# Two transformer blocks on one core: residual additions of seven rows on GpSimd, a leading weight chunk split in halves, and one copy moved to ScalarE

## The chip, the cores and the metric

The kernel runs on one core of a Trainium2 chip. The metric is the device time of one execution in microseconds (us). Before the change it is 1349.7 us, the median of three runs (1349.34 to 1349.88).

## What is computed

A residual stream x of 512 tokens by 1024 features goes through two blocks. Each block is a mixer and a feed-forward part, and both of them end and begin in the same way:

```python
x = x + gt_a * rms_norm(mix, g_mix_post)          # residual
h_ffn = modulate(rms_norm(x, g_ffn_pre), sh_f, sc_f)   # h * (1 + scale) + shift
ffn = conv_ffn(h_ffn, ...)
x = x + gt_f * rms_norm(ffn, g_ffn_post)
```

The first block mixes by retention and a Fourier transform, the second by a causal convolution and stick-breaking attention. All of it is fp32; the modulation vectors (shift, scale, gate) come from two matrix-vector products with 6144 columns each.

## The kernel before

Data is feature-major: a tile is 128 features by 512 tokens, and x (`xT`) is eight such tiles, k = 0 to 7. A matmul in fp32 precision is made of three rounded ones: each operand is split into a high part (`hH`, `WH`) and the rest (`hL`, `WL`). Weights come in a stream of chunks of 128 by 2048 into three slots. SP issues the load of a chunk when the matmuls of the chunk three places earlier are done. ScalarE makes `WH` (`split_hi`), VectorE makes `WL` (`split_lo`), and TensorE waits for `lo_done`. GpSimd issues the DMAs of the modulation weights (`ada_half`, two buffers, L335), which VectorE consumes in `ada_step`.

The change is about the three places, called boundaries here (m = 0, 1, 2), where one part's output y (eight tiles, written by TensorE into four banks in turn) is normed, added to x, and x is normed again as the input of the next part. The code takes the second norm's mean square from sums of y*y, (gain*y)^2 and gain*y*x, so that it needn't wait for the new x:

- In the last tiles of the output phase (`out_tile`) VectorE copies gain*y to `yT` (L1166), multiplies by x (L1169) and adds to three sums (L1174, L1178). For tile 7 it makes only gain*y*x (L1162) and then `yT` (L1163), behind ScalarE's square of the bank (L606). Between tiles 6 and 7 both engines split the second chunk of the next phase (`split_hi`, `split_lo` of c0+5 or c0+13), 2048 columns at once.
- TensorE's `late_stats` sums over features (L1521), spreads the first root to all partitions (L1528, bank 4), later the second root (L1528, bank 5), and between them runs matmuls whose result nobody reads (`keep_running`, L1782, bank 7). It first waits for `mod_read`.
- ScalarE makes the first root from bank 4 (`y_root`, L382 and L383) and, once VectorE has made `sxx` (L1195 to L1200), the second.
- VectorE's `boundary` then scales y by the first root, reading bank 4 (`scale_y`, L1185), and adds it to x (`add_x`, L1189). The loop over k runs: L1212 (x times gain times second root, reading bank 5, to `tmp1`), `scale_y(k + 2)`, `add_x(k + 1)`, then, after ScalarE has made `hH` of tile k (L647), L1218 for `hL`. At its end the third chunk is split in four parts (L837).
- TensorE's `lead` multiplies two chunks at once, tile by tile as `hH` and `hL` come: per k eight matmuls with `hH` (L1814, L1815) and four with `hL` (L1820). It first waits for both chunks (`have(c + 1)`).

Each engine runs its instructions in program order; the order above is written out by hand, with semaphores between engines.

Of the kernel before, what the change touches and what calls it, by code (L numbers as in the profile page):

```python
# [21 lines left out]
KT = D // P  # L22
# [12 lines left out]
CH = 2048  # L35
# [56 lines left out]
def build(nc, weights, ada, ada_later, x_t, ctx_t, vecs, rope, band, pos, csd, masks, sel, x_rows, gain_row, out):  # L92
# [4 lines left out]
    with stack:  # L97
# [221 lines left out]
        @block.gpsimd  # L319
        def _(pool):  # L320
            pool.dma_start(selT[:, :], sel).then_inc(s.sel_in, 16)
            nc.gpsimd.memset(csil_pair[:, :, :], 0.0).then_inc(s.const_set, 1)
            nc.gpsimd.memset(eps[:, :], EPS).then_inc(s.const_set, 1)
            nc.gpsimd.memset(ones[:, :], 1.0).then_inc(s.const_set, 1)
            nc.gpsimd.memset(lift[:, :], 0.0).then_inc(s.const_set, 1)
            nc.gpsimd.memset(gp3[:, :], 0.0).then_inc(s.const_set, 1)
            pool.wait_ge(s.const_set, 5)
            for q in range(4):
                nc.gpsimd.memset(lift[32 * q:32 * q + 1, q:q + 1], 1.0).then_inc(s.const_set, 1)

            pool.wait_ge(s.mod0_sum, ADA_FIRST)
            for a in range(STEPS):
                if a >= 2:
                    pool.wait_ge(s.ada_read, a - 1)
                pool.dma_start(ada_half[:, a % 2, :], ada_later[a]).then_inc(ada_in[a % 2], 16)  # L335

            for p in range(PAIRS):
                if p % 4 in (1, 2):
                    w = P * (p % 4 + 1)
                    for e in range(2):  # L340
                        pool.wait_ge(s.sp_lo, 2 * p + e + 1)
                        if p % 4 == 2:
                            pool.wait_ge(s.cum_sum, passed(p - 1) - 1 + e)
                        nc.gpsimd.tensor_tensor(spF[p % 2][:, e, P:w], spF[p % 2][:, e, P:w],
                                                spF[(p - 1) % 2][:, e, 0:w - P], add).then_inc(s.cum_sum, 1)

            pool.wait_ge(s.turned, 1)
            for q in range(4):
                pool.dma_start(gain_row.rearrange("(k q j) -> q k j", q=4, j=32)[q], gpT[32 * q:32 * q + KT, :])\
                    .then_inc(s.rows_out, 16)  # L350
            pool.wait_ge(s.rows_out, 64)
            pool.dma_start(gpB[:, :], gain_row.partition_broadcast(P)).then_inc(s.rows_in, 16)
            for k in range(KT):
                pool.wait_ge(s.turned, k + 2)
                blocks = xB[:, k % 4, :].rearrange("p (b j) -> p b j", j=32)
                for q in range(4):
                    at = slice(P * k + 32 * q, P * k + 32 * q + 32)
                    pool.dma_start(x_rows[:, at].rearrange("(b i) j -> i b j", i=32), blocks[32 * q:32 * q + 32, :, :])\
                        .then_inc(s.rows_out, 16)
                pool.wait_ge(s.rows_out, 64 * (k + 2))  # L360
            pool.wait_ge(s.mm_done, 16 * C_DOWN2)
            pool.dma_start(x_tok[:, :, :], x_rows.rearrange("(t p) c -> p t c", p=P)).then_inc(s.rows_in, 16)

        @block.scalar
        def _(act):
# [3 lines left out]
            def split_hi(c, width=CH):  # L369
                slot = c % SLOTS  # L370
                act.wait_ge(raw_in[slot], 16 * (c // SLOTS) + 16)
                A(WH[:, slot, 0:width], raw[:, slot, 0:width], ACT.Copy).then_inc(s.hi_done, 1)  # L372
# [224 lines left out]
            def out_squares(m, n, done_at):  # L597
# [9 lines left out]
                if n < KT - 1:  # L607
                    A(to[:, 1, :], b[:, :], ACT.Square, scale=gp[:, n:n + 1]).then_inc(s.zz_ready, 1)

            def out_phase(m, c0):  # L610

                pin_ln_exp()
                split_hi(c0 + 1)
                for p in range(4):
                    if p < 3:
                        split_hi(c0 + p + 2)
                    out_squares(m, 2 * p, done(c0 + p, 0, 2))
                    if p == 3:
                        split_hi(c0 + 5)
                    out_squares(m, 2 * p + 1, done(c0 + p, 1, 2))  # L620

            def down_phase(m, c0):
                pin_ln_exp()
                for p in range(4):
                    for j in range(3):
                        q = 3 * p + j
                        if q < 11:
                            split_hi(c0 + q + 2)
                    out_squares(m, 2 * p, done(c0 + 3 * p + 2, 0, 2))
                    if p == 3:  # L630
                        split_hi(c0 + 13)
                    out_squares(m, 2 * p + 1, done(c0 + 3 * p + 2, 1, 2))

            def y_root(m):
# [3 lines left out]
            def next_norm(m, c0):  # L638

                y_root(m - 1)  # L640
                act.wait_ge(s.sxx_ready, m + 1)
                inverse_root(xroot, sxx[:, :], 1.0 / D, s.xroot_ready)
                for k in range(KT):
                    if k == 4:
                        split_hi(c0 + 2)
                    act.wait_ge(s.norm_mul, m * KT + k + 1)
                    A(hH[:, k, :], tmp1[:, k % 4, :], ACT.Identity, bias=mod[:, SHIFT_AT[m] + k:SHIFT_AT[m] + k + 1])\  # L647
                        .then_inc(s.h_hi, 1)
# [173 lines left out]
        def _(dve):  # L822
# [333 lines left out]
            def out_tile(m, n, free0):  # L1156

                if n == KT - 1:
                    b = bank[Y_BANKS[m][n % 4]]
                    dve.wait_ge(s.yy_ready, m * KT + n + 1)  # L1160
                    dve.wait_ge(s.xy_added, 6 * m + 6)
                    STT(last_xy[m][:, :], b[:, :], gp[:, n:n + 1], xT[:, n, :], mult, mult).then_inc(s.xy_ready, 1)  # L1162
                    TS(yT[:, n, :], b[:, :], gp[:, n:n + 1], None, mult).then_inc(s.bank_free, 1)  # L1163
                    return
                dve.wait_ge(s.zz_ready, m * (KT - 1) + n + 1)
                TS(yT[:, n, :], bank[Y_BANKS[m][n % 4]][:, :], gp[:, n:n + 1], None, mult).then_inc(s.bank_free, 1)  # L1166
# [10 lines left out]
                        dve.wait_ge(s.xy_added, 6 * m + n - 1)  # L1177
                    TT_(sums[m][:, 2, :], sums[m][:, 2, :], xy, add).then_inc(s.xy_added, 1)  # L1178

            def boundary(m, c0):  # L1180

                r, r2, t = bank[4][:, :], bank[5][:, :], xsum

# [4 lines left out]
                    dve.wait_ge(s.y_scaled, KT * m + k + 1)  # L1188
                    TT_(xT[:, k, :], xT[:, k, :], yT[:, k, :], add).then_inc(s.x_new, 1)  # L1189

                at = SCALE_AT[m + 1]
                STT(gm[:, 0, :], mod[:, at:at + KT], 1.0, v(f"g{m + 1}", 0, KT), add, mult).then_inc(s.gm_ready, 1)
                dve.wait_ge(s.root_ready, m + 1)
                dve.wait_ge(s.zstat_done, m + 1)
                own.link(TT_(t, bank[5][:, 0:P], yroot, mult))  # L1195
# [4 lines left out]
                TS(sxx[:, :], sxx[:, :], 0.0, None, ALU.max).then_inc(s.sxx_ready, 1)  # L1200
                dve.wait_ge(s.y_spread, m + 1)
                scale_y(0)
                scale_y(1)
                add_x(0)
                dve.wait_ge(s.gm_ready, m + 1)
                dve.wait_ge(s.x_spread, m + 2)
                at = SHIFT_AT[m + 1]
                for k in range(KT):
                    dve.wait_ge(s.x_new, KT * m + k + 1)
                    if k >= 4:  # L1210
                        dve.wait_ge(s.h_lo, KT * (m + 1) + k - 3)
                    STT(tmp1[:, k % 4, :], xT[:, k, :], gm[:, 0, k:k + 1], r2, mult, mult).then_inc(s.norm_mul, 1)  # L1212
                    if k < KT - 2:
                        scale_y(k + 2)
                    if k < KT - 1:
                        add_x(k + 1)
                    dve.wait_ge(s.h_hi, KT * (m + 1) + k + 1)
                    STT(hL[:, k, :], tmp1[:, k % 4, :], mod[:, at + k:at + k + 1], hH[:, k, :], add, sub)\  # L1218
                        .then_inc(s.h_lo, 1)
                split_lo_parts(c0 + 2, m)  # L1220

            def out_phase(m, c0, free0, after, steps=(0, 0, 0, 0)):
                post_gain(m)
                split_lo(c0 + 1)
                for p in range(4):
                    if p < 3:
                        split_lo(c0 + p + 2)
                        ada_steps(steps[p])
                    out_tile(m, 2 * p, free0)
                    if p == 3:  # L1230
                        split_lo(c0 + 5)
                        if m == 0:
                            modulation(2, 8, 24)
                    out_tile(m, 2 * p + 1, free0)
                boundary(m, after)

            def down_phase(m, c0, free0, after):
                post_gain(m)
                for p in range(4):
# [6 lines left out]
                                modulation(4, 40, 48)  # L1246
                    out_tile(m, 2 * p, free0)
                    if p == 3:
                        split_lo(c0 + 13)
                    out_tile(m, 2 * p + 1, free0)  # L1250
                boundary(m, after)

            out_phase(0, C_OUT, B_OUT, C_UP, (1, 1, 0, 0))
            assert ada_next[0] == STEPS_UP, ada_next
# [215 lines left out]
        def _(pe):  # L1470
# [313 lines left out]
            def late_stats(m):  # L1784

                have((C_UP, C_U, C_UP2)[m])
                pe.wait_ge(s.mod_read, (2, 5, 6)[m])
                early_stats(m)
                pe.wait_ge(s.yy_ready, (m + 1) * KT)
                token_sums(4, odd_sq[m][:, 0, :], False, True).then_inc(s.ystat_done, 1)  # L1790
                pe.wait_ge(s.gp_squared, m + 1)
                token_sums(5, odd_sq[m][:, 0, :], False, True, gp_last[:, 0:1].to_broadcast([P, 32]))\
                    .then_inc(s.zstat_done, 1)
                keep_running(m, 2)
                pe.wait_ge(s.xy_ready, (m + 1) * KT)
                token_sums(6, last_xy[m][:, :], False, True).then_inc(s.xystat_done, 1)
                pe.wait_ge(s.const_set, 9)
                pe.wait_ge(s.root_ready, m + 1)
                spread(4, yroot).then_inc(s.y_spread, 1)
                keep_running(m, 4)  # L1800
                pe.wait_ge(s.xroot_ready, m + 2)
                spread(5, xroot).then_inc(s.x_spread, 1)
                keep_running(m, 5)

            def lead(c, banks, at):

                have(c + 1)
                for k in range(KT):
                    pe.wait_ge(s.h_hi, at + k + 1)
                    for j in range(2):  # L1810
                        for x in range(2):
# [378 lines left out]
```

## Time and profile before

| | |
|---|---|
| median of three runs | 1349.7 us |
| profiled execution, its own time | 1348.56 us |
| its span in the trace | 1346.8 us |
| PE busy | 1327.9 us, 99% |
| VectorE busy | 901.4 us, 67% |
| ScalarE busy | 526.4 us, 39% |
| GpSimd busy | 83.8 us, 6% |
| granted TensorE clock | 9 tenths or more of full speed in all 40 slices |

Engines are named PE (TensorE matmul), PEld (its weight load), DVE (VectorE), ACT (ScalarE), POOL (GpSimd) and SP. Matmul ends are modelled, so a busy PE is not PE at its peak. The three boundaries lie at about 264 to 295 us, 633 to 662 us and 974 to 1005 us of the span. What matters there is which engine is waited for last, and that is read from the timeline.

### The profile page before, as it was taken

To read this page: it belongs to the slowest core of one execution; us is meant where nothing else is said; L and a number is where in the kernel's file an instruction comes from. 1 tells how busy PE (TensorE), PEld (TensorE's weight loads), DVE (VectorE), ACT (ScalarE), POOL (GpSimd) and SP (SyncE) were. 2 spreads that over 40 slices of the span, in tenths; PEclk is the share of its full clock that TensorE was granted. 3 is DMA by queue.
4 is the path that set the end of the run, shared out by engine and by line. 5 is a ranking of instruction groups with operands and counts; after the bars stand their busy time and mean duration, and the time that the engine had idled before them with its cause. 6 is when DMAs were issued, how large, how long until landed. Compare 5 with 4: busy or idle time off the path is not lost.

```text
span 1346.8 us, 15738 instructions
## 1 busy us (share of the span) xinstructions
PE 1327.9 (99%) x6461; PEld 1077.6 (80%) x6461; DVE 901.4 (67%) x1126; ACT 526.4 (39%) x747; POOL 83.8 (6%) x148
## 2 busy tenths in 40 slices
PE   7999999999999999999999999999999999999998
PEld 4799688778888888887888777778878888888886
DVE  4787878988777777678758899766875433332224
ACT  4552444344334443222422666774333222222112
POOL 0000001000000001010000100000002220000000
PEclk9999999999999999999999999999999999999999
DMA  9543046324445555654123211112224332224331
GB/s 390 191 141 126 17 155 220 125 78 175 163 162 196 171 183 186 217 202 173 71 94 98 90 64 63 63 63 96 98 86 131 116 115 94 94 98 161 107 104 63
DMA packets 32887, 176.47 MB, mean 131 GB/s; under 512 B 4128, under 2 KB 4400, under 8 KB 17840
## 3 DMA queue, kind: packets, MB, share of 16 engines
q1 hardware_dynamic: 19440, 128.78, 26.7%
q0 software_dynamic: 13376, 46.69, 10.8%
q8 instruction: 51, 0.84, 0.3%
q14 instruction: 20, 0.16, 0.0%
HBM read 171.26 MB, written 4.20 MB: 130 GB/s over the span
## 4 chain that ended last, share of the span: by engine, by line
PE 90%; DVE 5%; issue 2%; ACT 2%; DMA 2%; SPq 0%; DVEq 0%; ACTq 0%
PE bank L1475 27%; PE bank L1477 26%; PE bank L1476 26%; PE bank L1814 2%; PE bank L1815 2%; PE bank L1820 2%; PE bank L1680 1%; DMA adaf<-ada 1%; PE bank L2010 1%; PE bank L1980 1%; DVE WL L830 1%; DVE sums L1174 1%; PE bank L1998 1%; PE bank L1997 1%; DMA raw<-weights 1%
## 5 line engine op out<-in xcount | busy, mean ns | idle before, releaser
L1475 PE MATMUL bank<-hH,WH 128*128 128x512 f32 x992 | 390.1, 393 | 0.9 <-DVE WL L830 0.6
L830 DVE TENSOR_TENSOR WL<-raw,WH 128x2048 fp32r<-128x2048 f32 x103 | 234.5, 2278 | 230.2 <-ACT WH L372 230.2
L1477 PE MATMUL bank<-hH,WL 128*128 128x512 f32 x992 | 386.4, 390 | 0.0
L1476 PE MATMUL bank<-hL,WH 128*128 128x512 f32 x992 | 386.2, 389 | 0.0
L372 ACT ACTIVATE WH<-raw 128x2048 fp32r<-128x2048 f32 x106 | 201.5, 1904 | 237.3 <-DMA raw<-weights 237.3
L1475 PEld LDWEIGHTS bank<-hH,WH 128*128 128x128 f32 x992 | 186.3, 188 | 42.6 <-issue 3.3
L1477 PEld LDWEIGHTS bank<-hH,WL 128*128 128x128 f32 x992 | 186.2, 188 | 39.6
L1476 PEld LDWEIGHTS bank<-hL,WH 128*128 128x128 f32 x992 | 186.3, 188 | 37.6 <-issue 0.2
L859 DVE SCALAR_TENSOR_TENSOR ada_acc<-ada_half,csil,ada_acc 128x1024 f32<-128x1024 f32 x70 | 89.7, 1281 | 6.4 <-DMA ada_half<-ada_later 3.8
L1307 DVE SCALAR_TENSOR_TENSOR cacc<-uT,vec,cacc 128x511 f32<-128x511 f32 (+29 forms) x120 | 83.3, 755 | 0.0
L335 POOL DMA_DIRECT2D ada_half<-ada_later x80 | 42.4, 530 | 571.8 <-DVE ada_acc L859 333.4
L1475 PE MATMUL bank<-GH,WH 128*128 128x512 f32 x176 | 68.7, 390 | 0.0
L1477 PE MATMUL bank<-GH,WL 128*128 128x512 f32 x176 | 68.5, 389 | 0.0
L1476 PE MATMUL bank<-GL,WH 128*128 128x512 f32 x176 | 68.5, 389 | 0.0
L1475 PE MATMUL bank<-WH,GH 128*128 128x512 f32 x176 | 68.5, 389 | 0.0
L1476 PE MATMUL bank<-WL,GH 128*128 128x512 f32 x176 | 68.5, 389 | 0.0
L1477 PE MATMUL bank<-WH,GL 128*128 128x512 f32 x176 | 68.5, 389 | 0.0
L806 ACT ACTIVATE GH<-tB 128x512 fp32r<-128x512 f32 x22 | 13.9, 632 | 88.5 <-DVE tB L1446 88.5
L1265 DVE SCALAR_TENSOR_TENSOR tB<-bank,vec,tB 128x504 f32<-128x504 f32 x22 | 16.4, 743 | 40.8 <-ACT tB L660 40.7
L660 ACT ACTIVATE tB<-bank,vec 128x512 f32<-128x512 f32 x22 | 17.2, 780 | 67.0 <-PE bank L1477 67.0
L1814 PE MATMUL bank<-hH,WH 128*128 128x512 f32 x96 | 37.6, 392 | 1.8 <-ACT hH L647 1.8
L1475 PEld LDWEIGHTS bank<-WH,GH 128*128 128x128 f32 x176 | 33.0, 188 | 6.9
(333 smaller groups left out, 2075.1 us busy)
## 6 DMA issues: line engine op xcount, KB each, us to landing
raw<-weights SPq DMA_DIRECT2D x108, 1024.0 KB, 4.9
ada_half<-ada_later POOLq DMA_DIRECT2D x80, 512.0 KB, 4.4
adaf<-ada SPq DMA_DIRECT2D x8, 1024.0 KB, 19.8
xT<-x_t SPq DMA_DIRECT2D x4, 512.0 KB, 5.7
x_rows<-xB POOLq DMA_DIRECT2D x32, 64.0 KB, 2.2
x_tok<-x_rows POOLq DMA_DIRECT2D x1, 2048.0 KB, 10.9
out_t<-x_tok SPq DMA_DIRECT2D x8, 256.0 KB, 2.0
ctxT<-ctx_t SPq DMA_DIRECT2D x1, 1024.0 KB, 28.6
```

The costliest lines, as they stand in the source:

```text
L335: pool.dma_start(ada_half[:, a % 2, :], ada_later[a]).then_inc(ada_in[a % 2], 16)
L372: A(WH[:, slot, 0:width], raw[:, slot, 0:width], ACT.Copy).then_inc(s.hi_done, 1)
L660: A(tmp[:, j, :], bank[2 * (t % 3) + x][:, :], ACT.Identity, bias=v("cb", x * FT + t), scale=v("cw", 2 * FT + x * FT + t)).then_inc(s.conv ...
L830: TT_(WL[:, slot, 0:width], raw[:, slot, 0:width], WH[:, slot, 0:width], sub).then_inc(s.lo_done, 1)
L859: ins = STT(ada_acc[:, :], w, c_col, ada_acc[:, :], mult, add)
L1307: STT(cacc[:, k, shift:L], uT[:, k, 0:L - shift], w, cacc[:, k, shift:L], mult, add)\
L1475: mm(o, lh, rh, start=start, stop=False, skip_group_check=skip)
L1476: mm(o, lh, rl, start=False, stop=False, skip_group_check=skip)
L1477: return mm(o, ll, rh, start=False, stop=stop, skip_group_check=skip)
L1814: mm(o, wh, hH[:, k, :], start=(k == 0), stop=False)
L1815: mm(o, wl, hH[:, k, :], start=False, stop=False)
L1820: ins = mm(bank[banks[j] + x][:, :], wh, hL[:, k, :], start=False, stop=(k == KT - 1))
```

## The change

It has four parts.

1. `add_x(k)` for k = 1 to 7 leaves VectorE and is issued by GpSimd (`residual(m)`), each behind `y_scaled` of its tile. `residual(0)` stands in GpSimd's queue behind the issue of the modulation DMA 25, `residual(1)` behind the last of them, `residual(2)` ahead of the DMAs of the gain row. VectorE keeps `add_x(0)`, now ahead of `scale_y(1)`.
2. The second leading chunk is split in halves: ScalarE makes both halves where it made the whole; VectorE makes half 0 between tiles 6 and 7 and half 1 in the loop at k = 2, ahead of `hL` of that tile. `lead` waits for half 0 at its start, for the whole at k = 4.
3. The copy `yT` of tile 7 goes to ScalarE, behind its first root, and VectorE waits for it at k = 5.
4. `gm` is made before tile 7; TensorE's wait for `mod_read` comes after the sums, and two of its filler matmuls are gone.

```diff
+            def residual(m):
+                for k in range(1, KT):
+                    pool.wait_ge(s.y_scaled, KT * m + k + 1)
+                    nc.gpsimd.tensor_tensor(xT[:, k, :], xT[:, k, :], yT[:, k, :], add).then_inc(s.x_new, 1)
...
                 pool.dma_start(ada_half[:, a % 2, :], ada_later[a]).then_inc(ada_in[a % 2], 16)
+                if a == STEPS_UP + 1:
+                    residual(0)
+            residual(1)
...
+            residual(2)
             pool.wait_ge(s.turned, 1)
...
+            def lead_hi(c):
+                slot = c % SLOTS
+                act.wait_ge(raw_in[slot], 16 * (c // SLOTS) + 16)
+                for half, ready in enumerate((s.hi_half, s.hi_done)):
+                    at = slice(CH // 2 * half, CH // 2 * half + CH // 2)
+                    A(WH[:, slot, at], raw[:, slot, at], ACT.Copy).then_inc(ready, 1)
...
                 y_root(m - 1)
+                n = KT - 1
+                act.wait_ge(s.xy_ready, m * KT)
+                A(yT[:, n, :], bank[Y_BANKS[m - 1][n % 4]][:, :], ACT.Identity, scale=gp[:, n:n + 1])\
+                    .then_inc(s.bank_free, 1)
                 act.wait_ge(s.sxx_ready, m + 1)
...
                     STT(last_xy[m][:, :], b[:, :], gp[:, n:n + 1], xT[:, n, :], mult, mult).then_inc(s.xy_ready, 1)
-                    TS(yT[:, n, :], b[:, :], gp[:, n:n + 1], None, mult).then_inc(s.bank_free, 1)
...
+            def lead_lo(m, c, half):
+                slot = c % SLOTS
+                at = slice(CH // 2 * half, CH // 2 * half + CH // 2)
+                if half:
+                    dve.wait_ge(s.hi_done, c + 1)
+                else:
+                    dve.wait_ge(s.hi_half, 2 + m + 1)
+                TT_(WL[:, slot, at], raw[:, slot, at], WH[:, slot, at], sub).then_inc(s.lo_done if half else s.lo_half, 1)
...
                 scale_y(0)
+                add_x(0)
                 scale_y(1)
-                add_x(0)
...
+                    if k == KT - 3:
+                        dve.wait_ge(s.bank_free, free0 + KT)
                     if k < KT - 2:
                         scale_y(k + 2)
-                    if k < KT - 1:
-                        add_x(k + 1)
+                    if k == 2:
+                        lead_lo(m, c0 + 1, 1)
                     dve.wait_ge(s.h_hi, KT * (m + 1) + k + 1)
...
                     if p == 3:
-                        split_lo(c0 + 5)
                         if m == 0:
                             modulation(2, 8, 24)
+                        next_gain(m)
+                        lead_lo(m, after + 1, 0)
...
-                pe.wait_ge(s.mod_read, (2, 5, 6)[m])
                 early_stats(m)
...
-                keep_running(m, 2)
+                pe.wait_ge(s.mod_read, (2, 5, 6)[m])
+                keep_running(m, 1)
...
-                keep_running(m, 4)
+                keep_running(m, 3)
...
-                have(c + 1)
+                have(c)
+                pe.wait_ge(s.lo_half, 2 + at // KT)
                 for k in range(KT):
+                    if k == 4:
+                        have(c + 1)
                     pe.wait_ge(s.h_hi, at + k + 1)
```

## Rows read from the trace of the kernel before

**Rows 1.** Timeline, boundary 1: start us, us, engine line op, operands, [idle before <-releaser].
```profile
632.12 2.29 DVE L830 TENSOR_TENSOR WL<-raw,WH 128x2048 fp32r<-128x2048 f32 x1
...
633.22 0.60 ACT L606 ACTIVATE odd_sq<-bank 128x512 f32<-128x512 f32 x1 [2.45 <-PE bank L1477]
...
634.32 0.74 DVE L1162 SCALAR_TENSOR_TENSOR last_xy<-bank,gp,xT 128x512 f32<-128x512 f32 x1
...
634.76 0.31 ACT L383 ACTIVATE rstd<-rstd 128x128 f32<-128x128 f32 x1
...
635.71 0.28 DVE L1195 TENSOR_TENSOR rstd<-bank,rstd 128x128 f32<-128x128 f32 x1
...
637.01 0.23 DVE L1200 TENSOR_SCALAR sxx<-sxx 128x128 f32<-128x128 f32 x1
...
638.07 1.16 PE L1528 MATMUL bank<-rstd,lift 128*128 128x128 f32 x8 [0.50 <-ACT rstd L383]
...
640.98 0.47 PE L1814 MATMUL bank<-hH,WH 128*128 128x512 f32 x1 [0.59 <-ACT hH L647]
```

**Rows 2.** Timeline, boundary 0, where the wait for the modulation lies.
```profile
264.05 0.60 ACT L606 ACTIVATE odd_sq<-bank 128x512 f32<-128x512 f32 x1 [2.88 <-PE bank L1477]
...
265.33 0.17 DVE L880 TENSOR_TENSOR mod<-bank,vec 128x16 f32<-128x16 f32 x1
...
269.04 0.23 DVE L1200 TENSOR_SCALAR sxx<-sxx 128x128 f32<-128x128 f32 x1
```

**Rows 3.** Timeline, boundary 2, the same line as in rows 1.
```profile
978.20 0.23 DVE L1200 TENSOR_SCALAR sxx<-sxx 128x128 f32<-128x128 f32 x1
```

**Rows 4.** Timeline, boundary 0, VectorE's loop over k.
```profile
276.41 0.74 DVE L1212 SCALAR_TENSOR_TENSOR tmp<-xT,gm,bank 128x512 f32<-128x512 f32 x1
...
277.07 0.68 DVE L1185 TENSOR_TENSOR yT<-yT,bank 128x512 f32<-128x512 f32 x1
...
278.27 0.74 DVE L1218 SCALAR_TENSOR_TENSOR hL<-tmp,mod,hH 128x512 fp32r<-128x512 f32 x1
...
286.50 0.74 DVE L1212 SCALAR_TENSOR_TENSOR tmp<-xT,gm,bank 128x512 f32<-128x512 f32 x1
...
288.03 0.75 DVE L1218 SCALAR_TENSOR_TENSOR hL<-tmp,mod,hH 128x512 fp32r<-128x512 f32 x1 [0.19 <-ACT hH L647]
```

**Rows 5.** Chain that ended last, boundary 0: start us, us, what.
```profile
273.01 0.47 PE bank L1814
...
275.10 0.92 PE bank L1820 x4
...
277.83 0.91 PE bank L1820 x4
```

**Rows 6.** Timeline, attention stage: GpSimd's additions of 256 columns beside VectorE.
```profile
769.63 3.19 POOL L344 TENSOR_TENSOR spF<-spF,spF 128x256 f32<-128x256 f32 x1 [5.66 <-DVE spL L1349]
769.95 2.28 DVE L830 TENSOR_TENSOR WL<-raw,WH 128x2048 fp32r<-128x2048 f32 x1
...
858.00 0.69 DVE L1409 TENSOR_TENSOR cacc<-cacc,rstd 128x512 f32<-128x512 f32 x1
...
865.28 0.56 DVE L1349 TENSOR_TENSOR spL<-spF,spH 128x384 fp32r<-128x384 f32 x1
...
865.76 0.55 DVE L1349 TENSOR_TENSOR spL<-spF,spH 128x384 fp32r<-128x384 f32 x1
865.92 0.99 POOL L344 TENSOR_TENSOR spF<-spF,spF 128x256 f32<-128x256 f32 x1 [9.14 <-DVE spL L1349]
866.23 1.23 DVE L1374 TENSOR_TENSOR lnsq<-lnsq 128x512 f32<-128x512 f32 x1
```

**Rows 7.** Timeline, attention stage: additions of 128 columns beside a cast from PSUM.
```profile
792.80 0.42 DVE L1349 TENSOR_TENSOR spL<-spF,spH 128x256 fp32r<-128x256 f32 x1
...
792.97 0.58 POOL L344 TENSOR_TENSOR spF<-spF,spF 128x128 f32<-128x128 f32 x1 [19.01 <-DVE spL L1349]
...
793.50 0.46 POOL L344 TENSOR_TENSOR spF<-spF,spF 128x128 f32<-128x128 f32 x1
```

More of the change, by code:

```diff
@@ L618, in out_phase @@
                     if p == 3:
-                        split_hi(c0 + 5)
+                        lead_hi(c0 + 5)
                     out_squares(m, 2 * p + 1, done(c0 + p, 1, 2))
@@ L630, in down_phase @@
                     if p == 3:
-                        split_hi(c0 + 13)
+                        lead_hi(c0 + 13)
                     out_squares(m, 2 * p + 1, done(c0 + 3 * p + 2, 1, 2))
@@ L1178, in out_tile, with next_gain, boundary @@
                     TT_(sums[m][:, 2, :], sums[m][:, 2, :], xy, add).then_inc(s.xy_added, 1)
-            def boundary(m, c0):
+            def lead_lo(m, c, half):
[6 more added lines that the diff above has]
+                TT_(WL[:, slot, at], raw[:, slot, at], WH[:, slot, at], sub).then_inc(s.lo_done if half else s.lo_half, 1)
+            def next_gain(m):
+                at = SCALE_AT[m + 1]
+                STT(gm[:, 0, :], mod[:, at:at + KT], 1.0, v(f"g{m + 1}", 0, KT), add, mult).then_inc(s.gm_ready, 1)
+            def boundary(m, c0, free0):
                 r, r2, t = bank[4][:, :], bank[5][:, :], xsum
@@ L1189, in add_x @@
                     TT_(xT[:, k, :], xT[:, k, :], yT[:, k, :], add).then_inc(s.x_new, 1)
-                at = SCALE_AT[m + 1]
-                STT(gm[:, 0, :], mod[:, at:at + KT], 1.0, v(f"g{m + 1}", 0, KT), add, mult).then_inc(s.gm_ready, 1)
                 dve.wait_ge(s.root_ready, m + 1)
@@ L1230, in out_phase @@
                     if p == 3:
-                        split_lo(c0 + 5)
                         if m == 0:
                             modulation(2, 8, 24)
+                        next_gain(m)
+                        lead_lo(m, after + 1, 0)
                     out_tile(m, 2 * p + 1, free0)
-                boundary(m, after)
+                boundary(m, after, free0)
             def down_phase(m, c0, free0, after):
@@ L1248, in down_phase @@
                     if p == 3:
-                        split_lo(c0 + 13)
+                        next_gain(m)
+                        lead_lo(m, after + 1, 0)
                     out_tile(m, 2 * p + 1, free0)
-                boundary(m, after)
+                boundary(m, after, free0)
             out_phase(0, C_OUT, B_OUT, C_UP, (1, 1, 0, 0))
```

## Prediction

> **What bounds the kernel now.** I read the page first: PE is busy 99% of the span, so only a place where PE waits can give time. The chain of waits shows three alike, the boundaries; the timeline around each is what counts. At boundary 1 [rows 1] the reader is to follow one chain: the square of tile 7 (starts 633.22, lasts 0.60), the last product L1162 (634.32), L1195 to L1200 on VectorE (635.71 to 637.01 plus 0.23), the second root on ScalarE, its spread on PE (638.07, 1.16), L1212, `hH`, and the first matmul of `lead` at 640.98. Behind that PE goes without a stop: one k of `lead` takes 277.83 - 275.10 = 2.73 us [rows 5]. VectorE's loop is just inside that: L1212, `scale_y` 0.66 later, an addition of about 0.60, `hL` 1.86 after L1212, and 0.66 more for `hL`, 2.52 us a k [rows 4].
>
> **Part 1: the chain ahead of `lead`.** Half of the 2.29 us split goes from ahead of tile 7. At boundary 1 VectorE is then free at 632.12 + 1.15 + 0.10 for `gm` = 633.4, and L1162 waits for the square: 633.82 + 0.06 = 633.88 in place of 634.32, done 634.62. L1195 no longer stands behind the copy of tile 7 but behind the first root: 634.76 + 0.31 + 0.03 = 635.10 in place of 635.71 [rows 1]. That is 0.61 us, and it carries to L1200, the second root and the spread. Boundary 2 has the same pattern (L1200 at 978.20) [rows 3]: 0.62 us. At boundary 0 the modulation's read L880 stood behind the split, at 265.33, and PE's sums and the first root behind it. With the wait moved, the square (264.05 + 0.60) is followed by the sums as in boundary 1: L1200 starts 637.01 - 635.71 = 1.30 after L1195, L1195 starts 635.10 - 633.22 = 1.88 after the square starts, so 264.05 + 1.88 + 1.30 = 267.23 against 269.04, a gain of 1.8 us [rows 1, 2]. The three sum to 3.0 us.
>
> What could take the place: ScalarE's copy of tile 7 costs some 0.70 us (my estimate, its square takes 0.60) from 635.10, and the second root is wanted at 637.27 - 0.61 = 636.66; so 0.86 us of cover is left, and the copy costs nothing. PE's first spread begins with the first root, 635.14, ends by 636.3, and VectorE wants it at 636.54; three fillers fit ahead of 637.46. VectorE's `scale_y(0)`, `add_x(0)`, `scale_y(1)`, now in series, end about 2.0 us later, 638.54, ahead of L1212 (638.72). Without these covers each would cost its own length. ScalarE's split in two instructions costs 0.2 us inside 2.45 or 2.88 us of idle time [rows 1, 2]: nothing. GpSimd's queue: DMA 26 waits for the tile loop behind boundary 0, the last modulation DMAs are issued before boundary 1, and the gain row comes from VectorE after boundary 2; nothing waits behind `residual`.
>
> **Part 2: the loop.** VectorE loses seven additions, and without other effects one k takes 1.53 us from L1212 to `hL` (288.03 - 286.50) and 0.66 for `hL`, 2.19 us [rows 4]. PE's 2.73 would still be the bound, and `hL`'s half split (1.15 us at k = 2) would fit.
>
> But the additions are not gone. The trace shows what a GpSimd addition does to a VectorE instruction with both inputs in SBUF: the 512-column addition L1374 lasts 1.23 us in place of the 0.69 of L1409, ending 0.55 after GpSimd's ends (866.91 to 867.46), and GpSimd's own began only when the L1349 ahead of it ended (866.31) [rows 6]. One stands still while the other runs. `hL` (from `tmp1` and `hH`) is such an instruction, and so are both split halves; L1212 and `scale_y` read one SBUF tensor and a bank. How long GpSimd holds: 0.60 us for 256 columns (866.31 to 866.91), 0.33 for 128 (793.22 to 793.55), so 512 columns give an estimate of 0.60 + 2 x 0.27 = 1.14 us [rows 6, 7]. No row shows 512 columns; the bounds are 0.69 (VectorE's speed) and 4 x 0.46 = 1.84.
>
> Who comes first decides. Count from the start of L1212(k). `scale_y(k + 2)` starts at 0.66 and ends at 1.34 [rows 4]; GpSimd follows the end of a VectorE instruction by 0.08 (865.84 to 865.92) [rows 6], so its addition is issued at 1.42. `hL(k)` is issued at 1.53. GpSimd leads by 0.11 us in every k from 0 to 5. It needs about 0.13 us before it begins (793.96 - 0.33 - 793.50) [rows 7], and VectorE needs part of 0.15, the excess of 0.69 over 512 columns, so this is close. I take GpSimd as first: it is issued first, and in rows 6 it goes ahead of L1374, issued 0.31 after it. The same rows hold the contrary case: at 769.63 GpSimd was issued 0.32 ahead of L830, yet lasted 3.19, behind all of L830's 2.28.
>
> If GpSimd is first, it ends at 1.55 + 1.14 = 2.69, `hL` at 3.24, and the next L1212 starts at 3.17: VectorE is the bound, 0.44 us a k above PE's 2.73. At k = 2 the half split holds till 2.48, GpSimd runs to 3.63, `hL` ends at 4.18, and the k takes 4.09: 1.36 above. First k: PE's own is some 0.2 longer (275.10 + 0.92 - 273.01 = 3.01 by the chain, 2.84 by the timeline), so only 0.25 is lost. A boundary loses 0.25 + 0.44 + 1.36 + 3 x 0.44 = 3.4 us, three 10.2, and with the 3.0 gained the change costs **7.2 us**.
>
> The Trainium skill, SBUF — State Buffer, section Who interferes with whom, says that a VectorE instruction with two SBUF inputs and a GpSimd one that reads SBUF exclude each other, and that whichever is issued first has the ports for its whole length. By that rule GpSimd is first and the time is the forecast below; by the row at 769.63 it may lose, and the time would be the first rival's.
>
> **How the numbers follow.** The profiled execution took 1348.56 us, 1.8 more than its span; 7.2 more is 1355.8. The median is 1.1 above the profiled one, so **1356.9 us**, slower by 0.5%. With the hold between 0.69 and 1.84 us a k changes by -0.45 to +0.70: the forecast's own range is 1348 to 1370, and 1354 to 1359 where the estimate holds within 0.15 us. Chance 0.58.
>
> **Rival A, VectorE first.** `hL` takes the ports from 1.53, GpSimd waits some 0.7 us and runs beside the next L1212 and `scale_y`, whose banks it doesn't touch; its sum is due a whole k later. A k takes 2.19, PE's 2.73 bounds, even with the split half and ScalarE's split at k = 4 (each delays VectorE by under 1.2 us, against 0.5 us of lead won in every k). The 3.0 us stay: 1346.7. For it: the row at 769.63 and the close race. Against it: 0.11 us of lead. Chance 0.27. It is the case on the other side, and decides where GpSimd begins over 0.11 us later than I read.
>
> **Rival B, mixed.** GpSimd is first in some k only, or only at k = 2 is VectorE's `hL` the first behind the half split. The latter takes 1.1 us from each boundary: 1353.6. If GpSimd wins no more than every second k, the lead VectorE gains in the others (0.54 each) covers most of the loss: 1348 to 1351. Together 0.15.
>
> **Rival C, the change doesn't shorten the chain**, since the spread or the copy is later than I read. It lowers the gain of 3.0 by under 1 us and is held in the ranges of the others.
>
> **Chances.** A measurement of this kernel can tell about 0.2%, 2.7 us, from no change. Rival A, 3.0 us faster, lies barely beyond: 0.22 of it faster, 0.05 the same. B gives 0.10 the same, 0.02 faster and 0.03 slower, the forecast 0.58 slower. So faster 0.24, same 0.15, slower 0.61. The range 1346.3 to 1359 takes in all three cases and leaves out a longer hold of GpSimd.
>
> **What would show it.** In the changed kernel, L1200's place should start 1.8, 0.6 and 0.6 us sooner after the last matmul of the phase. GpSimd's additions should show 1.3 us or more, `hL` of k = 0 to 5 about 1.7 us in place of 0.74, the first L1814 of k = 1 to 6 idle ahead of it 0.3 to 1.4 us, and a `lead` of about 25 us for 21.9. If `hL` shows 0.74 and GpSimd's additions about 2 us, rival A holds. The forecast is wrong too if a VectorE instruction that reads a bank and one SBUF tensor is held up: then every k costs more.

## The result, and the profile after

The changed kernel takes 1357.12 us (median of five runs, 1355.98 to 1357.71). Against runs of the kernel before on the same chip the ratio is 1.0058, with a 95% interval of 1.0044 to 1.0072: slower by 0.6%, about 7.8 us. The profiled execution has a span of 1354.6 us for 1346.8.

Two lines of the page of the changed kernel show where to look, and so do PE's waits in the lead (us in total, times, longest), first of the changed kernel, then of the kernel before:

```profile
PE 1333.4 (98%) x6455; PEld 1075.4 (79%) x6455; DVE 906.6 (67%) x1105; ACT 528.6 (39%) x753; POOL 113.9 (8%) x169
...
L335 POOL TENSOR_TENSOR xT<-xT,yT 128x512 f32<-128x512 f32 x21 | 29.8, 1420 | 185.3 <-DVE yT L1222 185.3
```

```profile
PE bank L1856 <- ACT hH L670: 3.1, 9, 0.6
PE bank L1862 <- DVE hL L1255: 1.7, 3, 0.6
```

```profile
PE bank L1814 <- ACT hH L647: 1.8, 3, 0.6
```

VectorE has 21 instructions less and GpSimd 21 more, and yet VectorE is busy 5 us longer. In the leads PE waits for `hH` in nine places where it waited in three, and three times for `hL`, for which it didn't wait there before.

The timeline of the changed kernel at boundary 0 answers rows 1, 2 and 4. The chain ahead of `lead`, from the square of tile 7:

```profile
262.99 1.22 DVE L1210 TENSOR_TENSOR WL<-raw,WH 128x1024 fp32r<-128x1024 f32 x1
264.22 0.60 ACT L617 ACTIVATE odd_sq<-bank 128x512 f32<-128x512 f32 x1 [2.78 <-PE bank L1516]
...
265.98 0.67 ACT L662 ACTIVATE yT<-bank,gp 128x512 f32<-128x512 f32 x1
266.10 0.29 DVE L1230 TENSOR_TENSOR rstd<-bank,rstd 128x128 f32<-128x128 f32 x1 [0.50 <-ACT rstd L394]
...
267.42 0.23 DVE L1235 TENSOR_SCALAR sxx<-sxx 128x128 f32<-128x128 f32 x1
```

L1235 (L1200 before) starts 3.20 us after the square where it started 269.04 - 264.05 = 4.99 after it [rows 2]: 1.8 us won. Then the loop over k, first k = 1, then k = 2 with the half split L1210, then the start of k = 3:

```profile
272.90 0.74 DVE L1247 SCALAR_TENSOR_TENSOR tmp<-xT,gm,bank 128x512 f32<-128x512 f32 x1
273.56 0.68 DVE L1222 TENSOR_TENSOR yT<-yT,bank 128x512 f32<-128x512 f32 x1
...
274.32 1.28 POOL L335 TENSOR_TENSOR xT<-xT,yT 128x512 f32<-128x512 f32 x1 [1.88 <-DVE yT L1222]
274.43 1.72 DVE L1255 SCALAR_TENSOR_TENSOR hL<-tmp,mod,hH 128x512 fp32r<-128x512 f32 x1 [0.20 <-ACT hH L670]
...
276.07 0.73 DVE L1247 SCALAR_TENSOR_TENSOR tmp<-xT,gm,bank 128x512 f32<-128x512 f32 x1
...
277.33 1.21 DVE L1210 TENSOR_TENSOR WL<-raw,WH 128x1024 fp32r<-128x1024 f32 x1
277.48 2.21 POOL L335 TENSOR_TENSOR xT<-xT,yT 128x512 f32<-128x512 f32 x1 [1.88 <-DVE yT L1222]
...
278.46 1.78 DVE L1255 SCALAR_TENSOR_TENSOR hL<-tmp,mod,hH 128x512 fp32r<-128x512 f32 x1
280.17 0.73 DVE L1247 SCALAR_TENSOR_TENSOR tmp<-xT,gm,bank 128x512 f32<-128x512 f32 x1
```

GpSimd's addition is issued 0.11 us ahead of `hL` (274.32, 274.43) and ends at 275.60; `hL` takes 1.72 us for 0.74 and ends at 276.15. One k takes 276.07 - 272.90 = 3.17 us, the k with the half split 280.17 - 276.07 = 4.10. L1247 and L1222, which read one SBUF tensor and a bank, are not held. At k = 0 an addition runs beside both, and all three take their usual time:

```profile
269.65 1.29 POOL L335 TENSOR_TENSOR xT<-xT,yT 128x512 f32<-128x512 f32 x1 [23.80 <-DVE yT L1222]
269.73 0.75 DVE L1247 SCALAR_TENSOR_TENSOR tmp<-xT,gm,bank 128x512 f32<-128x512 f32 x1 [0.17 <-PE bank L1567]
270.39 0.68 DVE L1222 TENSOR_TENSOR yT<-yT,bank 128x512 f32<-128x512 f32 x1
```

All runs can be laid out by three landmarks in each boundary: the square of tile 7, the first matmul of `lead`, and the end of its last group of four. "Gap" is from the first to the second, "lead" from the second to the third, in us of the profiled execution:

| kernel | gap 0, 1, 2 | lead 0, 1, 2 | span |
|---|---|---|---|
| before | 8.96, 7.76, 7.76 | 22.05, 22.05, 22.01 | 1346.8 |
| changed | 7.16, 7.16, 7.16 | 25.59, 25.60, 25.61 | 1354.6 |
| e1_adds_on_dve | 7.16, 7.16, 7.17 | 22.53, 22.51, 22.53 | 1345.8 |
| e2_after_hl | 7.16, 7.17, 7.16 | 22.06, 22.04, 22.03 | 1344.9 |
| e3_half_add | 7.16, 7.16, 7.16 | 22.65, 22.62, 22.60 | 1345.3 |
| e4_only_adds | 8.37, 7.76, 7.76 | 24.67, 24.66, 24.65 | 1354.0 |
| e5_delays | 7.16, 7.16, 7.16 | 25.63, 25.83, 25.98 | 1355.3 |
| e6_copy | 7.17, 7.16, 7.17 | 22.17, 22.22, 22.18 | 1345.8 |
| e7_write_only | 7.17, 7.16, 7.17 | 22.04, 22.01, 22.01 | 1344.8 |
| e8_copy_back | 7.21, 7.20, 7.22 | 22.01, 22.05, 22.01 | 1343.3 |
| e9_tie | 7.16, 7.17, 7.16 | 22.33, 22.30, 22.30 | 1345.5 |
| e10_only_adds_after_hl | 8.36, 7.76, 7.76 | 22.04, 22.01, 22.03 | 1346.2 |

For the changed kernel the gaps give back 1.80 + 0.60 + 0.60 = 3.0 us and the leads take 3.54 + 3.55 + 3.60 = 10.7; together 7.7 of the span's 7.8. What lies between the boundaries takes the same in both to 0.1 us; the stretch ahead of the first is 0.2 us longer. Each row of the table is one execution, and the gap of boundary 0 in the kernel before depends on the execution, as is shown further down.

### The profile page after: what moved, and what is told of

The parts are those of the page before. It is cut to its first block, busy times and chain, and to the rows that moved or that the text cites. A ratio compares the mean times of both kernels' runs of the same rounds, so it can differ in the third digit from the quotient of the medians.

```text
span 1354.6 us, 15738 instructions
## 1 busy us (share of the span) xinstructions
PE 1333.4 (98%) x6455; PEld 1075.4 (79%) x6455; DVE 906.6 (67%) x1105; ACT 528.6 (39%) x753; POOL 113.9 (8%) x169
## 4 chain that ended last, share of the span: by engine, by line
PE 84%; DVE 8%; ACT 4%; issue 2%; DMA 1%; SPq 0%; DVEq 0%; ACTq 0%
PE bank L1514 26%; PE bank L1515 26%; PE bank L1516 26%; DVE hL L1255 1%; DVE tmp L1247 1%; DMA adaf<-ada 1%; PE bank L1719 1%; ACT hH L670 1%; DVE ada_acc L882 1%; DVE WL L853 1%; PE bank L2052 1%; PE bank L2022 1%; ACT WH L383 1%; PE bank L2040 1%; PE bank L2039 1%
## 5 line engine op out<-in xcount | busy, mean ns | idle before, releaser
L853 DVE TENSOR_TENSOR WL<-raw,WH 128x2048 fp32r<-128x2048 f32 x100 | 227.6, 2278 | 230.6 <-ACT WH L383 230.5
L383 ACT ACTIVATE WH<-raw 128x2048 fp32r<-128x2048 f32 x103 | 195.7, 1903 | 235.9 <-DMA raw<-weights 235.8
L335 POOL TENSOR_TENSOR xT<-xT,yT 128x512 f32<-128x512 f32 x21 | 29.8, 1420 | 185.3 <-DVE yT L1222 185.3
```

Source lines behind the costliest of these rows:

```text
L335: nc.gpsimd.tensor_tensor(xT[:, k, :], xT[:, k, :], yT[:, k, :], add).then_inc(s.x_new, 1)
L853: TT_(WL[:, slot, 0:width], raw[:, slot, 0:width], WH[:, slot, 0:width], sub).then_inc(s.lo_done, 1)
```

## The experiments

**e1_adds_on_dve: the other three parts alone.**

```diff
-                if a == STEPS_UP + 1:
-                    residual(0)
-            residual(1)
-            residual(2)
...
                         scale_y(k + 2)
+                    if k < KT - 1:
+                        add_x(k + 1)
                     if k == 2:
```

> All parts of the change but the first: add_x(1) to add_x(7) are back on VectorE, in their old place behind scale_y(k + 2); GpSimd adds nothing. Theory (the loss is hL held up by GpSimd's additions): the chain ahead of lead keeps its 3.0 us; a k of VectorE's loop takes 2.52 us again, plus 1.15 us for the half split at k = 2, which the 0.2 us a k won on PE by then doesn't cover: about 0.3 us lost in each boundary. 1347.7 us, ratio to before 0.9985; hL shows 0.74 us everywhere. Rival (the halves, the copy on ScalarE or the moved waits are what costs): 1354 us or more.

Measured: 1347.64 us against 1348.45 for the kernel before, ratio 0.9995 (0.9987 to 1.0004). The gaps keep their 7.16 us, and the leads lose 0.5 us each, for the 0.3 expected. The rival is out by far: without GpSimd's additions none of the 7.8 us is left. The ratio was expected lower by 0.001; that is looked at below.

**e2_after_hl: GpSimd always second.**

```diff
                     pool.wait_ge(s.y_scaled, KT * m + k + 1)
+                    if k >= 2:
+                        pool.wait_ge(s.h_lo, KT * (m + 1) + k - 1)
                     nc.gpsimd.tensor_tensor(xT[:, k, :], xT[:, k, :], yT[:, k, :], add)...
```

> The changed kernel, but GpSimd's addition k waits, from k = 2 on, until hL(k - 2) is done; so GpSimd always comes second. Theory: each hL takes 0.74 us, a k of VectorE's loop 2.2 us, lead is bound by PE at 2.73 us a k and lasts 22.0 us for 25.6, and the 3.0 us of the chain remain: 1346.7 us, ratio 0.9978. Rival (GpSimd's additions are simply too slow, and L1247 waits for them): GpSimd starts even later here, so lead stays at 25 us or more and the time at 1357 us or above.

Measured: 1347.04 us, ratio to before 0.9989 (0.9980 to 0.9998): 1.5 us faster, and the 0.9978 expected lies just outside the interval. The timeline of this kernel, boundary 0, k = 1:

```profile
272.27 0.74 DVE L1249 SCALAR_TENSOR_TENSOR tmp<-xT,gm,bank 128x512 f32<-128x512 f32 x1
272.50 1.29 POOL L337 TENSOR_TENSOR xT<-xT,yT 128x512 f32<-128x512 f32 x1 [1.23 <-DVE hL L1257]
...
273.81 0.75 DVE L1257 SCALAR_TENSOR_TENSOR hL<-tmp,mod,hH 128x512 fp32r<-128x512 f32 x1 [0.19 <-ACT hH L672]
...
274.48 0.74 DVE L1249 SCALAR_TENSOR_TENSOR tmp<-xT,gm,bank 128x512 f32<-128x512 f32 x1
```

The same additions, just as long, now begin beside L1249 and end (273.79) when the next `hL` is issued. Only the half split at k = 2 still meets the end of one: it takes 1.35 us for 1.22. A k takes 2.21 us and lead 22.05. In the profile, one added wait on the helping engine takes all of the 10.7 us of the leads away; between the two ratios, 1.0058 and 0.9989, lie 9.3 us. The additions' own slowness cost nothing.

**e3_half_add: half the length of the hold.**

```diff
-   nc.gpsimd.tensor_tensor(xT[:, k, :], xT[:, k, :], yT[:, k, :], add)
+   nc.gpsimd.tensor_tensor(xT[:, k, 0:256], xT[:, k, 0:256], yT[:, k, 0:256], add)
```

> The changed kernel with GpSimd adding columns 0 to 255 of the seven tiles only; the residual is left out for the other 256 tokens in tiles 1 to 7. Theory (the loss is the length of the hold): the hold falls from 1.14 to 0.60 us, hL takes about 1.2 us, a k 2.6 us, inside PE's 2.73; only k = 2 with the half split still costs some 0.4 us a boundary: 1347.9 us, ratio 0.9987. Rival (a fixed cost of each GpSimd instruction or semaphore delays hL): the loss hardly falls, 1355 us or more.

Measured: 1348.03 us, ratio 0.9999 (0.9989 to 1.0008). Its timeline:

```profile
273.35 0.73 POOL L335 TENSOR_TENSOR xT<-xT,yT 128x256 f32<-128x256 f32 x1 [1.88 <-DVE yT L1222]
273.47 1.17 DVE L1255 SCALAR_TENSOR_TENSOR hL<-tmp,mod,hH 128x512 fp32r<-128x512 f32 x1 [0.20 <-ACT hH L670]
```

`hL` falls from 1.72 to 1.17 us with an addition that is 0.55 shorter: the loss is the length of the hold, not a fixed cost. A k takes 2.61 us (274.55 - 271.94), inside PE's 2.73. With the half split at k = 2 a lead is 22.6, a loss of 0.6 us for the 0.4 expected. The ratio was expected at 0.9987, a little below the interval.

**e4_only_adds: the first part alone.** The kernel before, with `residual(m)` on GpSimd and `add_x(1)` to `add_x(7)` gone from VectorE. One more line changes place: `add_x(0)` stands ahead of `scale_y(1)`, as in the changed kernel. It lies under cover: the gaps of boundaries 1 and 2 stay at 7.76 us.

```diff
+            residual(0) / residual(1) / residual(2)   # at the same places in GpSimd's queue
...
                 scale_y(0)
+                add_x(0)
                 scale_y(1)
-                add_x(0)
...
-                    if k < KT - 1:
-                        add_x(k + 1)
```

> The kernel before with only the seven additions moved to GpSimd: the split of the second chunk whole, the copy on VectorE, TensorE's waits and fillers as before. Theory: no gain in the chain, and in lead 0.25 us at k = 1 and 0.44 at k = 2 to 6, 2.45 us a boundary: 7.4 us slower, 1357.1 us, ratio 1.0055, lead 24.5 us in each boundary. Rival (the loss needs the half split inside the loop): about 1350 us, ratio 1.000.

Measured: 1356.57 us, ratio 1.0061 (1.0049 to 1.0074). Leads of 24.66 us, 2.6 more than before, 7.9 in sum. So the two ways in which the loss grows are apart now: 2.6 us a boundary from `hL` alone, 0.9 more from the half split that queues in the same loop (25.6 in the changed kernel).

**e5_delays: small memsets ahead of GpSimd's addition.**

```diff
+                    for e in range(m if k >= 2 else 0):
+                        at = 8 + 6 * (m - 1 + e) + k - 2
+                        nc.gpsimd.memset(gp3[:, at:at + 1], 0.0)
```

> The changed kernel with small GpSimd memsets of one column ahead of each addition from k = 2 on: none in boundary 0, one in boundary 1, two in boundary 2. A memset of that size takes about 0.1 us, so the addition is issued 1.42, 1.53 and 1.63 us after L1247, and hL at 1.53. Theory (who comes first decides, and GpSimd leads by 0.11 us): boundary 0 as in the changed kernel, hL 1.72 us and lead 25.6 us; boundary 2 tips over to VectorE, hL 0.74 us and lead about 22.1 us; boundary 1 lies on the edge. Rival (GpSimd wins whenever both are near, or wins over an instruction already running): all three leads stay at 25.6 us or grow with the memsets.

Measured: leads of 25.63, 25.83 and 25.98 us, 1357.06 us in one run. That boundary 2 would tip over was wrong, and the timeline says why: the memsets overlap, and two of them put the addition off by only 0.09 us (issued 986.57, from 986.48).

```profile
986.48 0.13 POOL L337 MEMSET gp<- 128x1 f32 x2 [0.21 <-DVE yT L1225]
986.57 1.29 POOL L338 TENSOR_TENSOR xT<-xT,yT 128x512 f32<-128x512 f32 x1
986.61 1.79 DVE L1258 SCALAR_TENSOR_TENSOR hL<-tmp,mod,hH 128x512 fp32r<-128x512 f32 x1 [0.19 <-ACT hH L673]
```

A lead of 0.04 us is still enough for GpSimd, and `hL` is held as long as GpSimd ends later. This run alone leaves open whether issue order decides or GpSimd wins every close race.

**e9_tie: the same event releases both.** It takes up that question. The edit is the wait below, with the memsets of e5 behind it.

```diff
+                    if k >= 2:
+                        pool.wait_ge(s.h_hi, KT * (m + 1) + k - 1)
```

> The changed kernel with GpSimd's addition k waiting, from k = 2 on, for ScalarE's hH(k - 2) as well, the same event that releases hL(k - 2); behind that wait stand no, one and two one-column memsets in boundaries 0, 1 and 2, each some 0.05 us by the last look. So GpSimd is issued at about the same time as hL, 0.05 and 0.1 us after it. Theory (the one that is issued first takes the reads): the lead turns from 25.6 us to about 22.1 us between one boundary and the next, where GpSimd's issue falls behind VectorE's; hL is 1.7 us or 0.75 us, nothing between. Rival (GpSimd wins every close race, VectorE's claim coming late in its instruction): all three boundaries stay at 25.6 us or more.

Measured: leads of 22.33, 22.30 and 22.30 us, 1347.29 us in one run. Neither side of the expectation holds as written: all three boundaries turned, since GpSimd answers ScalarE's event 0.12 us later than VectorE does, without any memset. What theory and rival disagree on is settled all the same:

```profile
271.55 0.75 DVE L1260 SCALAR_TENSOR_TENSOR hL<-tmp,mod,hH 128x512 fp32r<-128x512 f32 x1 [0.19 <-ACT hH L675]
...
271.67 1.79 POOL L340 TENSOR_TENSOR xT<-xT,yT 128x512 f32<-128x512 f32 x1 [0.44 <-ACT hH L675]
```

Issued 0.12 us behind `hL`, GpSimd is the one that stands still: 1.79 us for 1.29, while `hL` takes its 0.75. Between 0.04 us ahead (e5) and 0.12 us behind the order turns; where in between was not tried.

One k in each boundary did not turn, k = 2. There VectorE is still at its half split when ScalarE's event comes, so GpSimd's addition is issued ahead of `hL` again, and `hL` is held as in the changed kernel:

```profile
276.07 1.98 POOL L340 TENSOR_TENSOR xT<-xT,yT 128x512 f32<-128x512 f32 x1 [0.40 <-ACT hH L675]
...
276.82 1.78 DVE L1260 SCALAR_TENSOR_TENSOR hL<-tmp,mod,hH 128x512 fp32r<-128x512 f32 x1
```

That is where the leads lose the 0.26 to 0.27 us by which they are above e2's: PE's k = 2 and k = 3 take up to 2.88 us for 2.72, all others what they take in e2.

**e6_copy and e7_write_only: what is held.** GpSimd's addition gives way to a copy (one tensor read) and to a memset (none read).

```diff
-   nc.gpsimd.tensor_tensor(xT[:, k, :], xT[:, k, :], yT[:, k, :], add)
+   nc.gpsimd.tensor_copy(xT[:, k, :], yT[:, k, :])     # e6
+   nc.gpsimd.memset(xT[:, k, :], 1.0)                  # e7
```

> The changed kernel with GpSimd copying yT to xT in place of adding (the sum with the old x is left out for tiles 1 to 7): one tensor read in place of two. Theory (any GpSimd instruction that reads SBUF holds hL for its length): hL of k = 0 to 5 is still held, for as long as the copy lasts; if a copy takes half of the addition's 1.29 us, hL takes about 1.2 us and lead 22.6 us. Rival (only the second tensor read is in VectorE's way): hL 0.74 us, lead 22.1 us.

> The changed kernel with GpSimd filling tiles 1 to 7 of xT with ones by memset in place of adding (the residual and the old x are left out there): it reads nothing and writes 512 columns. Theory (what is shared is the way in which a second SBUF tensor is read): hL takes 0.74 us everywhere, the half split 1.22 us, lead 22.1 us. Rival (any GpSimd instruction on SBUF holds VectorE): hL is held by the memset's length, some 0.4 us.

Measured: 1347.86 us with the copy and 1346.76 with the memset, one run each. First the copy, then the memset, each at boundary 0:

```profile
272.19 0.61 POOL L335 COPY xT<-yT 128x512 f32<-128x512 f32 x1 [0.89 <-DVE yT L1222]
272.31 1.03 DVE L1255 SCALAR_TENSOR_TENSOR hL<-tmp,mod,hH 128x512 fp32r<-128x512 f32 x1 [0.19 <-ACT hH L670]
```

```profile
271.59 0.53 POOL L335 MEMSET xT<- 128x512 f32 x1 [0.98 <-DVE yT L1222]
271.73 0.75 DVE L1255 SCALAR_TENSOR_TENSOR hL<-tmp,mod,hH 128x512 fp32r<-128x512 f32 x1 [0.19 <-ACT hH L670]
```

The copy ends at 272.80 and `hL` 0.54 us later, at 273.34, as behind an addition; the memset, which runs beside `hL` for 0.39 us, leaves it at 0.75. Nor does VectorE hold the memset: beside the half split (275.85, 1.22 us) one issued at 275.99 takes 0.53 us as ever. So one read tensor is enough to hold VectorE, and a write is not. This is what the page SBUF — State Buffer of the Trainium skill says under Who interferes with whom, of both. Leads are 22.2 and 22.0 us; the copy was a little shorter than half the addition (0.61), so its 1.03 and 22.2 lie under the 1.2 and 22.6 expected.

**e8_copy_back: what of the other parts gave the chain's gain.** The kernel of e2, with two parts undone:

```diff
     STT(last_xy[m][:, :], b[:, :], gp[:, n:n + 1], xT[:, n, :], mult, mult).then_inc(s.xy_ready, 1)
+    TS(yT[:, n, :], b[:, :], gp[:, n:n + 1], None, mult).then_inc(s.bank_free, 1)
...
+                pe.wait_ge(s.mod_read, (2, 5, 6)[m])
                 early_stats(m)
```

> The kernel in which GpSimd's additions wait for hL(k - 2), with two more parts undone: the copy of tile 7 is on VectorE again, behind its last product, and TensorE again waits for mod_read ahead of its sums. Theory: the copy on VectorE ends 0.1 us after the first root, so the time from the last square to lead grows from 7.16 to 7.26 us in each boundary and no more; the wait for mod_read costs nothing, since the modulation's read now stands ahead of the half split, and boundary 0 shows the same 7.26. Rival (the copy's move is what the chain's gain comes from): 7.7 us. Rival (the wait is): 8 us or more in boundary 0 alone.

Measured: gaps of 7.21, 7.20 and 7.22 us, 1345.11 us in one run. The copy's move to ScalarE is worth 0.05 us a boundary, the moved wait nothing. What is left of the gain has not been taken apart by a run of its own, but VectorE's rows of boundary 1 show where it lies: the square, the last product and L1195's place start at 630.85, 631.48 and 632.80, in the kernel before at 633.22, 634.32 and 635.71. The product comes 0.47 us sooner behind the square (the half split) and L1195 0.07 us sooner behind the product (`gm` no longer stands between them). At boundary 0 the modulation's read, now ahead of the split, adds to it. The two fillers that are gone were not what was waited for in boundary 1: in the kernel before PE stood idle behind them for 0.50 us, waiting for the second root [rows 1].

**e10_only_adds_after_hl: the offload without the collision.** The kernel of e4, with e2's wait.

> The kernel before with only the seven additions moved to GpSimd, each from k = 2 on waiting for hL(k - 2). Theory: hL is no longer held, a k of VectorE's loop takes 2.2 us in place of 2.52, but PE's 2.73 was the bound already, so the move gives nothing: gaps of 7.76 us in boundaries 1 and 2, leads of 22.05 us, the time of the kernel before, ratio 1.000 within 0.001. Rival (taking work off VectorE is worth something by itself): leads below 22 us and a ratio of 0.998 or less.

Measured: 1348.55 us against 1348.16, ratio 1.0003 (0.9994 to 1.0013), leads of 22.04, 22.01 and 22.03. Taking seven additions off VectorE is worth nothing here, since PE's 2.73 us a k was the bound. The gap of boundary 0 is 8.36 us, as in e4 (8.37), for the 8.96 of the kernel before, though nothing ahead of the boundary is changed in either.

## Why the prediction was right, point by point

- **The chain ahead of lead, 3.0 us.** Right in the profile: 1.80, 0.60 and 0.60. Its covers held: ScalarE's copy ends at 266.65 where the second root is wanted at 267.68, 1.0 us of cover for 0.86; `scale_y(1)` ends at 269.56, L1247 starts at 269.73. But the 1.8 of boundary 0 is in part the execution's and not the change's. How far VectorE is behind there varies: it goes on from tile 6's sums between 0.78 and 1.52 us ahead of the square, 0.92 in the profiled execution of the kernel before, 1.51 and 1.52 in e4 and e10, whose code is the same up to there, 1.52 in the changed kernel, 0.92 in e1, 0.78 in e6. With the whole split this goes into the gap (8.96 against 8.37 and 8.36); with the half split it doesn't (7.16 to 7.21 in nine executions). So the change is worth 1.2 to 1.8 us at boundary 0 and 2.4 to 3.0 us in sum, and the runs don't say where in between the mean lies. For e2 that makes a ratio of 0.9982 to 0.9978 (measured 0.9989, 0.9980 to 0.9998), which speaks for the lower end; for e1, with 1.5 us lost in its leads, 0.9993 to 0.9989 (measured 0.9995, 0.9987 to 1.0004).
- **The hold, 1.14 us for 512 columns.** Right: 1.28 to 1.29 us with its start, `hL` ends 0.55 us behind it, a k of 3.17 us as worked out. e3 gives the slope: 256 columns less, 0.55 us less, 2.1 ns a column.
- **GpSimd first.** Right, with the 0.11 us of lead that was read from [rows 4, 6], in k = 0, 1, 3, 4 and 5 of each boundary. This was the step with the least under it. e5 and e9 bear it out: it holds down to 0.04 us and turns when GpSimd is behind. Behind the half split at k = 2, where the same question was open, GpSimd went first in all three boundaries. The contrary row, GpSimd ahead of L830 by 0.32 us and yet behind it, is no accident. It comes back in all twelve profiled executions, always at that place, with GpSimd 0.30 to 0.32 us ahead and its addition at 3.19 or 3.20 us. In the changed kernel, with a later place of the same shape beneath it at which GpSimd does go first:

```profile
774.50 3.19 POOL L354 TENSOR_TENSOR spF<-spF,spF 128x256 f32<-128x256 f32 x1 [5.66 <-DVE spL L1388]
774.82 2.27 DVE L853 TENSOR_TENSOR WL<-raw,WH 128x2048 fp32r<-128x2048 f32 x1
...
806.82 0.99 POOL L354 TENSOR_TENSOR spF<-spF,spF 128x256 f32<-128x256 f32 x1 [7.99 <-DVE spL L1388]
807.13 1.21 DVE L1346 SCALAR_TENSOR_TENSOR cacc<-uT,vec,cacc 128x491 f32<-128x491 f32 x1
```

  At both places GpSimd is issued while a two-tensor VectorE instruction (L1388) still runs, and the next one follows 0.31 or 0.32 us later. Why the split passes GpSimd and the other doesn't stays open. That the one issued first goes first is shown for `hL`, not for every pair, and a race behind a running instruction was a real risk for k = 2.
- **PE's loss, 3.4 us a boundary.** 3.54, 3.55 and 3.60. VectorE's part is exact: from L1247 of k = 0 (269.73) to that of k = 6 (289.68) it takes 19.95 us, against 5 x 3.17 + 4.09 = 19.94. The terms add to 3.37 us before rounding, so 0.17 to 0.23 us a boundary are missing. 0.14 of it is PE's restart, which the sum left out. The k behind a stop takes PE longer by itself: k = 0 takes 2.81 to 2.84 us in the kernel before, and k = 6 of the changed kernel, which starts after a stop and then runs through, takes 2.86 for 2.72 (2.73 by the chain), with a first matmul of 0.50 us for 0.39:

```profile
291.22 0.50 PE L1856 MATMUL bank<-hH,WH 128*128 128x512 f32 x1
...
294.08 0.39 PE L1856 MATMUL bank<-hH,WH 128*128 128x512 f32 x1
```

- **The sum.** Two terms are off, and both make the forecast too low: the gain is too high by up to 0.6 us, the loss too low by 0.5 in all. Corrected they make 10.7 less 3.0 to 2.4, 7.7 to 8.3 us, beside 7.4 by the medians and 7.8 by the ratio, whose interval is 5.9 to 9.7. The forecast of 7.2 us is inside too. That it comes within 0.3 us of the median is luck, with an interval of almost 4 us; what bears it out is the agreement term by term.
- **The rivals.** Rival A's condition, VectorE first, did not hold in the changed kernel. e2 and e9 brought it about, and the leads came down to 22.0 to 22.3 us as it says; e9 also shows its GpSimd additions of about 2 us (1.79). Its 3.0 us of gain is above the 1.5 us measured for e2 (0.3 to 2.7). Rival B did not occur: GpSimd was first in every k. Rival C did not either: the gaps became shorter by what was read, and spread and copy stayed under cover.

## What to carry to other kernels

Before work is moved to GpSimd, list the VectorE instructions that run beside it and read two SBUF tensors: each can stand still for the whole length of GpSimd's. For `hL` the order in which the two are issued decided who pays; for a whole-chunk split it didn't, so look in the trace at the very pair. Where GpSimd's result has slack, let it wait for the VectorE instruction it would collide with; here one wait took away all of the 10.7 us that the leads had lost. And ask first whether the relieved engine is the bound: VectorE was at 2.52 us beside PE's 2.73, so the offload could give nothing (e10), and e2 owes its 0.1% to the order ahead of the lead, the half split above all.

## What the runs showed of the hardware

- A GpSimd instruction that reads one SBUF tensor holds a two-tensor VectorE instruction as one that reads two does (e6: `hL` 1.03 us beside a copy of 0.61); one that only writes doesn't (e7: 0.75 beside a memset of 0.53).
- Against `hL`, a margin of 0.04 us in issue is enough for GpSimd to go first, and 0.12 us is enough for VectorE (e5, e9). Against the whole-chunk split in the attention stage 0.30 to 0.32 us were not enough for GpSimd, in all twelve executions. GpSimd follows the end of a VectorE instruction by 0.08 us (274.24 to 274.32 in the changed kernel) and ScalarE's event 0.12 us later than VectorE does (e9).
- A GpSimd memset of one column shows 0.10 us but puts the next instruction off by only some 0.05 (e5).
- The k of a lead in which PE starts after a stop takes it 2.81 to 2.87 us even where it then runs through, for 2.72 otherwise (k = 0 of the kernel before, k = 6 of the changed kernel and of e4).
